# Taking the input projections of a hybrid attention layer out of the attention, in seven-product pairs, and filling the attention with gate columns

## The reference, cut to what matters

```python
h = _rmsnorm(x, norm_mix_g[l])
proj = h @ w_in[l]
a_q, a_k, a_v, b_q, b_k, b_v, c_q, c_k, c_v, c_f, gates = jnp.split(proj, splits, axis=-1)
...
o_a = _diff_attention(...)          # 4 heads of 2 x 64, values of 128
o_b = _chunk_band_attention(...)    # 8 heads of 64, a band of 576 keys
o_c = _forgetting_attention(...)    # 8 heads of 64, causal
g = jax.nn.sigmoid(gates).reshape(b_, s_, N_BRANCH, D_MODEL)
merged = (g[:, :, 0] * (o_a @ w_br_a[l]) + g[:, :, 1] * (o_b @ w_br_b[l]) + g[:, :, 2] * (o_c @ w_br_c[l]))
x = x + merged @ w_out[l]
h = _rmsnorm(x, norm_ffn_g[l])
gt, up = jnp.split(h @ w_gate_up[l], 2, axis=-1)
x = x + (jax.nn.silu(gt) * up) @ w_down[l]
```

## Time and profile before

| | us |
|---|---|
| median of 3 runs | 1864.05 (1863.99 to 1865.76) |
| the profiled execution | 1865.28 |
| its span, first to last instruction | 1863.2 |
| PE busy | 1822.7 (98%) |
| DVE busy | 1253.0 (67%) |
| ACT busy | 878.3 (47%) |
| POOL busy | 297.0 (16%) |
| attention, from its first scores | 75 to 764 |
| gates in the merge block | 764 to 990 |
| branch tiles | 990 to 1125 |

### The profile page before, as it was taken

How to read it: one execution, slowest core, us unless ns; L and a number is a source line. 1 busy time by engine, 2 the same in 40 slices (tenths; PEclk the granted TensorE clock), 3 DMA queues, 4 the chain that set the end, 5 groups by cost and what they waited for, 6 DMA issues and landing times. The chain is left out here.

```text
span 1863.2 us, 25932 instructions
## 1 busy us (share of the span) xinstructions
PE 1822.7 (98%) x9046; PEld 1535.8 (82%) x9046; DVE 1253.0 (67%) x2359; ACT 878.3 (47%) x1679; POOL 297.0 (16%) x297
## 2 busy tenths in 40 slices
PE   6999999999999999999999999999999999999998
PEld 4888888888888888788888888887888888888886
DVE  5467666667667777685555776787766777676676
ACT  5555655677666777533333221263323232344444
POOL 2202212111111110033220000012232323200011
PEclk9999999999999999999999999999999999999999
DMA  8432323132231220334236562134565567469522
GB/s 235 134 88 58 90 70 82 38 82 57 79 91 46 57 85 35 102 113 136 91 102 221 159 206 98 46 147 159 194 201 182 207 228 243 146 225 409 198 95 90
DMA packets 189623, 248.06 MB, mean 133 GB/s; under 512 B 9684, under 2 KB 132692, under 8 KB 186952
## 3 DMA queue, kind: packets, MB, share of 16 engines
q1 hardware_dynamic: 187432, 246.60, 40.8%
q10 hardware_dynamic: 2080, 0.04, 0.1%
HBM read 172.09 MB, written 67.44 MB: 129 GB/s over the span
## 5 line engine op out<-in xcount | busy, mean ns | idle before, releaser
L214 PE MATMUL ps<-h_hi,w_hi 128*128 128x512 f32 x884 | 360.0, 407 | 4.9 <-PEq L622 1.8
L216 PE MATMUL ps<-h_hi,w_lo 128*128 128x512 f32 x884 | 346.3, 392 | 0.0
L215 PE MATMUL ps<-h_lo,w_hi 128*128 128x512 f32 x884 | 346.1, 391 | 0.0
L214 PEld LDWEIGHTS ps<-h_hi,w_hi 128*128 128x128 f32 x884 | 166.9, 189 | 37.8 <-issue 2.7
L216 PEld LDWEIGHTS ps<-h_hi,w_lo 128*128 128x128 f32 x884 | 166.4, 188 | 36.5
L215 PEld LDWEIGHTS ps<-h_lo,w_hi 128*128 128x128 f32 x884 | 167.1, 189 | 29.1
L792 POOL TENSOR_TENSOR w_lo<-w_raw,w_hi 128x256 fp32r<-128x256 f32 x138 | 102.1, 771 | 549.4 <-ACT w_hi L819 514.8
L994 DVE CUSTOM_DVE_ANT_0 probs_bc<-ps,bias 128x640 f32<-128x640 f32 (+7 forms) x128 | 90.5, 707 | 66.3 <-PE ps L1152 28.2
L215 PE MATMUL ps<-down_ring_w,down_ring_a 128*128 128x512 f32 x308 | 120.0, 389 | 0.0
L216 PE MATMUL ps<-down_ring_w,down_ring_a 128*128 128x512 f32 x308 | 120.0, 389 | 0.0
L214 PE MATMUL ps<-down_ring_w,down_ring_a 128*128 128x512 f32 x308 | 119.9, 389 | 0.0
(11 more groups left out here) (356 smaller groups left out, 4424.7 us busy)
## 6 DMA issues: line engine op xcount, KB each, us to landing
w_raw<-in_w_in SPq DMA_DIRECT2D x52, 512.0 KB, 5.2
w_raw<-in_w_gate_up SPq DMA_DIRECT2D x44, 512.0 KB, 3.9
k_stack<-k_stack SPq DMA_DIRECT2D x24, 512.0 KB, 5.5
gates_scratch<-gate_sigmoid SPq DMA_DIRECT2D x24, 512.0 KB, 3.5
gate_in<-gates_scratch SPq DMA_DIRECT2D x24, 512.0 KB, 3.7
down_rows<-in_w_down SPq DMA_DIRECT2D x11, 1024.0 KB, 7.1
hidden_scratch<-hidden_stage SPq DMA_DIRECT2D x22, 512.0 KB, 4.8
weight_sums_scratch<-weight_sums SPq DMA_DIRECT2D x11, 1024.0 KB, 4.9
```

Of the source, the lines that this page charges most:

```text
L214: nc.tensor.matmul(out, w_hi, x_hi, start=first, stop=False)
L215: nc.tensor.matmul(out, w_hi, x_lo, start=False, stop=False)
L216: return nc.tensor.matmul(out, w_lo, x_hi, start=False, stop=last)
```

## The change

- A new block, `block_project`, stands between norm and attention. It projects slab 3 plain and slabs 4 to 35 in 16 seven-product pairs. All results but those of unit 0 go to DRAM (`qkv_hi`, `qkv_lo`), through three rotating buffers `out_hi`, `out_lo` of 128 x 512. `block_norm` projects slabs 0 to 2, and DVE makes `t1` to `t3` there.
- The pair loop is new. The raw weights of one pair fit (`w_raw` slots 0 and 1), not of two. The products have seven PSUM banks instead of four.
- In the attention each unit gets its keys, queries and values from DRAM, 13 transfers (12 of 64 x 1024, one of 128 x 1024). The pieces between the steps are two plain gates a unit, 16 pieces; in the last unit 12. Raw gates, not sigmoids, are stored.
- In `block_merge` half a gate is left (24 matmuls). The sigmoid is taken when a gate is read back.
- Counted: plain slabs 42 to 28, pairs 9 to 16.

Cut to its core:

```diff
-PIECES_AT = [
-    [2, 2, 2, 2, 1, 1, 1, 1, 0, 0, 2, 1, 1, 1, 1, 2, 0],
...
-LAST_PIECES_AT = [0, 1, 0, 1, 0, 1, 0, 1, 0, 1, 0, 1, 0, 1, 1, 0, 0]
+PIECES_AT = [1, 1, 1, 1, 0, 1, 1, 1, 1, 0, 0, 1, 1, 1, 1, 0, 0]
+EVAC_AT = {1: 0, 4: 1, 9: 2, 16: 3}
+SPLIT_AT = {3: 1, 10: 2}
+LAST_PIECES_AT = [1, 0, 1, 0, 1, 0, 1, 0, 1, 0, 1, 0, 1, 0, 1, 0, 0]
...
+        block_project(nc, ps, keep, scratch, w_in_k)
         block_attention(nc, ps, keep, scratch, w_in_k, w_br_b)
...
+            for part in range(T_PARTS):
+                combine([(1, h12[0]), (0, h11[0]), (1, h12[1]), (0, h11[1])], part, 3 * part, t1_sum)
+            dve.wait_ge(t_sums, 6)
...
             dve.wait_ge(c_turned, 1)
             nc.vector.tensor_copy(keep["c_col"][:, :], bank(ps, C_BANK, TT * C_HEADS)).then_inc(c_out, 1)
...
+            for f in range(PROJECT_PAIRS):
+                sp.wait_ge(low, PRODUCTS * f + A_2 + 1)
+                sp.wait_ge(summed, 4 * (f + 1))
+                if f + 1 < PROJECT_PAIRS:
+                    load_a(f + 1)
+                    sp.wait_ge(low, PRODUCTS * (f + 1))
+                    load_b(f + 1)
...
+                outs = outs_of(f)
+                for name in ("b_late", "a_early", "b_early", "a_late"):
+                    store(outs[name])
...
+            def w_high(f, n):
...
+            def pair(f):
...
+                prepare(A_1, SUM_1)
+                prepare(SUM_2, SUM_3)
+                act.wait_ge(joined, JOINS * f + B_LATE)
+                take(outs["b_late"])
+                act.wait_ge(joined, JOINS * f + A_EARLY)
+                take(outs["a_early"])
+                prepare(A_2, B_2)
+                act.wait_ge(joined, JOINS * f + B_EARLY)
+                take(outs["b_early"])
+                prepare(SUM_4)
...
+                act.wait_ge(joined, JOINS * f + A_LATE)
+                take(outs["a_late"])
...
+            def w_low(f, n):
+                if n in (SUM_1, SUM_2):
+                    dve.wait_ge(summed, 4 * f + (2 if n == SUM_1 else 4))
...
+            def pair(f):
...
+                prepare(A_1)
+                ready(SUM_2)
+                dve.wait_ge(first_out, f + 1)
+                nc.vector.tensor_tensor(up_sum, first_sum, bank(ps, BANK_OF[SUM_2]), ALU.add).then_inc(joined, 1)
+                prepare(SUM_1)
+                ready(SUM_3)
+                add(last_sum, up_sum, SUM_3, U_DONE)
+                add(up_sum, up_sum, SUM_1, X_DONE)
+                add(gate_sum, last_sum, SUM_1, X_DONE)
+                prepare(SUM_2, SUM_3)
+                take_low(outs["b_late"])
+                ready(A_2)
+                add(first_sum, first_sum, A_2, U_DONE)
+                prepare(A_2)
+                take_low(outs["a_early"])
+                ready(B_2)
+                add(last_sum, last_sum, B_2, B_LATE)
+                prepare(B_2)
+                take_low(outs["b_early"])
+                ready(SUM_4)
+                add(up_sum, up_sum, SUM_4, V_DONE)
+                prepare(SUM_4)
...
+                take_low(outs["a_late"])
```

More of the change, by code:

```diff
@@ L678, in block_attention @@
         pv_bank = bank(ps, 7)
-        def proj_bank(unit, g):
-            if isinstance(unit, int) and unit in (0, UNITS):
-                return bank(ps, (0, 1, 2, 3, 5, 6)[g] if unit == 0 else 6)
-            return bank(ps, PROJ_BANKS[g])
         def pv_half(g):
@@ L893, in unit_body @@
                 c = counts(b, it, du)
-                slab = 3 * (c["unit"] + 1)
                 turns = turns_of(b)
@@ L1097, in unit_body @@
                             o_out_bc(c, (s - 3) // 2)
-                    if not project and s == STEPS:
-                        dve.wait_ge(w_hi_done, LAST_SLAB + 4)
-                        nc.vector.tensor_tensor(w_lo[:, 0, :, :], w_raw[:, 0, :, :], w_hi[:, 0, :, :].bitcast(F32),
-                                                ALU.subtract).then_inc(keep["gate_w_split"], 1)
-            for g in range(4):
-                project_low(0, g, 0)
             dve.wait_ge(mask_made, 2)
@@ L1335, in block_merge @@
-        BANK_OF = (0, 2, 1, 3, 0, 3, 2)
-        U, X, V, B_LATE, A_EARLY, B_EARLY, A_LATE = range(1, JOINS + 1)
-        SIG_ORDER = {"b_late": 1, "a_early": 2, "b_early": 3, "a_late": 4}
-        flat2 = lambda ap: ap.rearrange("p k n -> p (k n)")
-        split_n = lambda ap: ap.rearrange("p (k n) -> p k n", n=P)
-        loaded_a, loaded_b = ((flat2(w_raw[:, n, :, :]), sig_in[:, n, :]) for n in range(2))
-        def raw(f, n):
-            a, b = loaded_a[f % 2], loaded_b[f % 2]
-            if n in (SUM_1, SUM_2, SUM_3):
-                at = (SUM_1, SUM_2, SUM_3).index(n)
-                return keep["bias"][:, 0, at // 2, at % 2 * HALF:(at % 2 + 1) * HALF]
-            return {A_1: a[:, 0:HALF], A_2: a[:, HALF:D], SUM_4: b[:, 0:HALF], B_2: b[:, HALF:D]}[n]
@@ L1431, in _ @@
-            store(1)
-            sp.wait_ge(g_split, 3)
-            load_gate(5)
-            sp.wait_ge(sig_done, 6)
-            store(2)
-            sp.wait_ge(g_split, 4)
-            load_b(0)
-            sp.wait_ge(sig_done, 8)
-            store(3)
-            sp.wait_ge(g_split, 5)
-            load_a(0)
-            sp.wait_ge(summed, 1)
-            load_a(1)
-            load_b(1)
-            for q in (4, 5):
-                sp.wait_ge(sig_done, max(sig_count(q, half) for half in range(2)))
-                store(q)
@@ L1468, in _ @@
+            load_branch(1)
+            load_branch(2)
+            sp.wait_ge(keep["heads_stored"], 16 * (UNITS + 1))
+            sp.wait_ge(gate_ready, 1)
             sp.wait_ge(b_split, 1)
             load_branch(3)
+            sp.wait_ge(o_lo_done, 4)
+            for u in range(2):
+                load_c(u)
             sp.wait_ge(c_loaded, 32)
+            sp.wait_ge(o_lo_done, TT)
             for u in range(2, UPB):
                 load_c(u)
-            sp.wait_ge(product, ALL_PRODUCTS)
@@ L1474, in _ @@
-            for q in range(2):
-                sp.wait_ge(stored[q], STORED_FROM[q] + 16 * (TILES // 2))
             for q in range(TILES):
@@ L1892, in turn @@
                 last.then_inc(turned, 1)
-            for q, half in PLAIN:
-                gate(q, half)
-            for f in range(GATE_PAIRS):
-                pair(f)
+            last_gate()
             for q in range(TILES):
```

954 lines of the change are left out of this document (487 added, 467 removed), and 5 rows, old and new, of tables (EVAC_AT, PIECES_AT).

## The result

The changed kernel takes 1978.0 us (median of 4 runs, 1974.0 to 1981.0), the kernel before 1864.6: a ratio of 1.061, 95% interval 1.0585 to 1.0627. The forecast was 1903, with 1868 to 1930 as its range; the sign was right and the size was not. The profiled execution took 1974.0, its span is 1972.2, so 109.0 more than before where the sum said 39.4. The stages are windows between the first instructions of the blocks, and for the last unit its first read of scores; the second column is the prediction's own sum, stage by stage, against that span.

A forecast was written before the change was run, and what follows sets the result against it. PE's order of matmuls was taken as the bound: 84 saved matmuls gave −19.0 us, new waits and the last unit's gain brought the sum to +39.4 on 1865.3, so a median of 1903 us, range 1868 to 1930.

The forecast's parts named there:

- Attention, +11: 11 attention units: fewer pieces reopen half of the small holes, 1 us a unit, +11 us; bounds 0 and 51.
- Last unit, −5.5: Last attention unit: 12 pieces, four ahead of the first turn, leave about 5.5 of its 11 us not PE work: −5.5.
- The pair loop, +30.5: block_project's pair loop: loads, sums and joins take 22.2 or 21.0 us a turn where PE needs 19.05: +30.5; bounds +3, +45.
- the ring: Pair loop: closed chain of loads, POOL's sums, DVE's remainders and joins, last result, next loads; 22.2 or 21.0 us.
- Start of the pairs, +5.3: Start of block_project's pairs: PE waits for the product needing t4 until 31.5 us after the block's start: +5.3 us.
- End of norm, +7.4: End of block_norm: PE waits 6.5 us against 0.8 before, +5.7, plus 1.7 for a half-clock stretch: +7.4 us.
- End of pairs, +8.7: Behind the last pair product: a 7.0 us wait until PE restarts, plus 1.7 for half clock: +8.7 us.
- Merge, +1: block_merge: second half of the heads lands about when PE ends the half gate, +1 us; reading back raw gates costs nothing.
- The pairs did not keep PE's pace: Rival for the pair loop: seven banks and slack absorb the loads, so pairs keep PE's pace; 1873 us, chance 0.20.
- the waits were not covered: Rival for the whole kernel: all new waits are covered and PE runs from start to end; 1842 us, chance 0.12.
- The starving attention: Rival for the attention: gate weights rounded too late, up to 3.6 us more a unit, 40 in all; 1943 us, chance 0.10.

The follow-up runs named there:

- e5_end_pieces: Changed kernel with two of the 16 pieces moved from steps 12 and 14 to step 15 in each of 11 attention units: 1950.8 us, −27.3.
- e8_all: Changed kernel with new piece tables, joins ahead of weight blocks, t3/t4 sums moved to POOL/DVE in block_project, C heads rounded later: 1885.2 us, ratio to before 1.011.
- e1_tables: Changed kernel with the same number of attention pieces at other steps, last unit's at odd steps: 1947.0 us, −31.0, ratio to before 1.042.
- e3_ring: Changed kernel with DVE and ACT doing a pair's joins and results before the next pair's weight blocks: 1938.7 us, −39.3, ratio 1.038.
- e4_norm_merge: Changed kernel with 10 of 16 norm-block sums left out and branch C heads rounded one tile later in block_merge: 1968.0 us, −10.0.
- e2_half_fill: Changed kernel with every attention piece doing 3 of its 6 matmuls, gates incomplete: 1914.1 us.
- e6_a_table: e1_tables plus a piece table of its own for branch A: 1938.1 us, ratio to before 1.039, 9 below e1_tables.
- e7_more_fill: e1_tables with each piece 9 matmuls instead of 6, gates wrong: 2065.3 us, 118 more than e1_tables.

## Why the prediction was wrong in size

- **Attention, +11: the step that failed**, as "I take half of the small holes, 1 us a unit". It measured +57 (576.0 for 518.7, some 2 of it the half clock that I had put down to the end of the pairs). The step took its price from what was idle before, and let the removed pieces go as if they had stood evenly. The new table takes both pieces away from step 15, where the last heads pass through ACT and DVE. The numbers were in the diff, and the waits at the ends of the last unit showed what stands open without them. Moving two pieces back gave 24 us (e5_end_pieces), the other steps 13 more (539.0 in e8_all), and 20 stayed: 6 us each in branches B and C (1.6 to 2 a unit), 2 in A, and 6 ahead of the first unit's scores.
- **Last unit, −5.5**: measured 57.7 for 50.7. Of 12 pieces the eight behind the values stood at even steps, beside the products with the values, and none at the end. With the odd steps it took 53.0 (e1_tables). I counted its pieces and not their steps.
- **The pair loop, +30.5**: the mechanism was right and shown by e3_ring, which opened the ring by order alone. Its length was 22.1, where five turns of 22.2 and eight of 21.0 make 21.5, and it cost 34.9 us, the length by which e3_ring shortens the block. Two slips in its working: 918.06 − 915.43 is 2.63 and not 2.65, and with 13 turns of 0.8 more the upper bound is +41 and not +45.
- **Start of the pairs, +5.3**: a wait of 6.8 for `t4`, and half clock around its end, which the sum did not have. (The text says four products ahead of it; its 26.8 counts five, and the trace has five.) It stands from 111.1 to 121.3 in the trace, and PE works in the last 6 us of it: about 3 lost.
- **End of norm, +7.4**: PE's restart is 6.9 late (81.5 for 63.7 + 10.9), and the half-clock stretch is 10.2 us long, not 3.4; some 3 us are lost in it, not 1.7: 9.7.
- **End of pairs, +8.7**: a hole of 6.3 and half clock from PE's restart at 452.2 to 455.8, 8.1 together. Right.
- **Merge, +1**: measured 6.7. The wait for the C heads stands in ACT's order ahead of a sigmoid and of branch weights; I had looked at the time at which the heads land, not at what is queued behind the wait. e4_norm_merge and e8_all (149.0, +2.9) show both parts of it.
- **Rivals.** The pairs did not keep PE's pace and the waits were not covered. The starving attention had the right size (40 us) and the wrong mechanism: its 1943 was nearer than my own number, for a reason that it did not name.

What the runs did not take apart is the 12 us in B and C that stay with the best of these tables, and the holes in the third unit of B (last section).

## What to carry to other kernels

Filling work is priced by its place. Before a piece is taken out, list the waits that it covers, step by step, and price each as open, with the half clock behind it; an average per unit misled here. Where a stream must wait (for a load, for a sum), ask what stands behind that wait in program order and put the work that others wait for ahead of it: that one reordering was worth 35 us in its block, 39 in the median, with no other resource.

## What the runs showed of the hardware

- A hole of 2 us in PE's work can bring a stretch of half clock, not every one does. In the changed kernel the granted clock fell for 3.4 us behind each of the waits of 2.0 us at the ends of the four units of A, 1.2 to 1.4 us after PE had resumed; behind the four of 1.7 at the ends of units in B it fell once, behind the three of 1.9 in C once. In e3_ring and e4_norm_merge the first of the four waits in A had none. With the shorter holes of e5_end_pieces (1.0 at most at the ends of A) it never fell in the 11 units (clock 1.00). At waits of 6 to 7 us the stretches were 6.8 or 10.2 us long and began before PE had resumed. Over the span 84.8 us were granted at half, in e8_all 24.5. The prediction had carried 3.4 us over to every hole.
- POOL and DVE do not only slow each other; these rows fit with taking turns. Two remainders on DVE and two sums on POOL at the start of e8_all, DVE from 79.02 and POOL from 79.61:

```profile
74.87 4.77 POOL L786 TENSOR_TENSOR norm_t_sum<-norm_t_sum,h_hi 128x1024 f32<-128x1024 f32 x2 [4.61 <-POOLq L244]
79.61 6.72 POOL L786 TENSOR_TENSOR norm_t_sum<-norm_t_sum,h_lo 128x1024 f32<-128x1024 f32 x2
```
```profile
79.02 5.04 DVE L929 TENSOR_TENSOR proj_t_lo<-norm_t_sum,proj_t_hi 128x1024 fp32r<-128x1024 f32 x2
```

  The first row is two such POOL operations beside DVE work of another kind: 4.77 us. Two remainders with no POOL beside them take 2.35 (at 96.41 of the same trace). One after the other that is 7.1; both are done at 86.33, 7.3 us after the first began. The Trainium skill ("SBUF — State Buffer", section "SBUF: two separate sides") says that the two exclude each other for a whole instruction when the DVE operation has two SBUF inputs and the GpSimd operation reads SBUF; these rows agree. It would explain why PE still waits 6.9 us at the start of the pairs in e8_all, with sums moved from DVE to POOL, where the changed kernel waits 6.8; no run took that apart.
- In the seventh unit, the third of branch B and the start of the second pass of its loop, DVE is idle for 3.0 to 3.4 us and the profile names no releaser; all twelve kernels have this, the one before too. In e1_tables, e2_half_fill, e3_ring and e6_a_table a second such hole of 4.5 to 4.8 us follows, and the unit is up to 7 us longer than its neighbours; e5_end_pieces, e7_more_fill and e8_all don't have it. So a comparison between two of these kernels can hold some us that come from neither table nor order. What the hole is stays open.
